# Differential attention: halving the softmax difference first and turning it with transposing DMAs instead of TensorE

## What is computed

```
sc = einsum('bqhtd,bkhtd->bhtqk', qi, k) * HEAD_DIM ** -0.5
p = softmax(where(mask, sc, -inf), axis=-1)
attn = p[:, :, 0] - lam * p[:, :, 1]
o = einsum('bhqk,bkhe->bqhe', attn, v)
```

## Time and profile before

| | us |
|---|---|
| median of 3 runs (lowest to highest) | 1940.49 (1938.78 to 1941.45) |
| the profiled execution, its own time | 1941.98 |
| its span, first to last instruction | 1940.2 |
| granted TensorE clock, mean | 0.999 of full |
| PE busy | 1914.1 (99%) |
| DVE busy | 1180.9 (61%) |
| ACT busy | 996.3 (51%) |
| POOL busy | 389.1 (20%) |

### The profile page before, as it was taken

One profiled execution on the slowest core, in us unless ns is written; L12 is line 12 of the kernel. 1 busy time (PEld: TensorE's weight loads), 2 busy tenths in 40 slices (PEclk: granted clock), 3 DMA queues, 4 the chain that ended last, 5 costly groups with the idle time before them and its releaser, 6 DMA issues.

```text
span 1940.2 us, 28236 instructions
## 1 busy us (share of the span) xinstructions
PE 1914.1 (99%) x11272; PEld 1044.9 (54%) x11272; DVE 1180.9 (61%) x1555; ACT 996.3 (51%) x1924; POOL 389.1 (20%) x266
## 2 busy tenths in 40 slices
PE   7999999999999999999999999999999999999998
PEld 4446755455455665544454576554554556655443
DVE  6677555587436877644367765655872477775432
ACT  5674454465324666533356644544662256665321
POOL 0212011142212232111001130112331222321110
PEclk9999999999999999999999999999999999999999
DMA  6224223343334443233222242233333443332421
GB/s 190 86 87 153 98 98 109 98 117 96 103 103 126 125 126 109 88 130 137 66 66 87 77 163 94 103 109 91 111 104 109 125 115 105 114 109 88 156 93 44
DMA packets 204525, 208.98 MB, mean 108 GB/s; under 512 B 28688, under 2 KB 193514, under 8 KB 204394
## 3 DMA queue, kind: packets, MB, share of 16 engines
q1 hardware_dynamic: 204394, 207.17, 33.9%
HBM read 181.91 MB, written 2.16 MB: 95 GB/s over the span
## 4 chain that ended last, share of the span: by engine, by line
PE 91%; DVE 3%; issue 2%; ACT 1%; DMA 1%; POOL 1%; SPq 0%; DVEq 0%; POOLq 0%; ACTq 0%
PE PS L558 89%; DVE X L1315 1%; PE PS L750 1%; PE PS L666 1%; DVE wsp L1312 1%; DMA stage<-w_in 1%; PE PS L798 0%; PE PS L806 0%; POOL X L1672 0%; PE PS L836 0%; DMA X<-X 0%; DVE Y L1312 0%; DVE Y L1471 0%; ACT Y L1210 0%; DVE M L1312 0%
## 5 line engine op out<-in xcount | busy, mean ns | idle before, releaser
L558 PE MATMUL PS<-hT,wsp 128*128 128x512 f16 (+2 forms) x4968 | 1085.7, 376 | 1.0 <-ACT hT L966 1.0
L558 PEld LDWEIGHTS PS<-hT,wsp 128*128 128x128 f16 x4968 | 479.1, 98 | 556.4 <-issue 11.9
L1312 DVE SCALAR_TENSOR_TENSOR wsp<-stage,wsp 128x2048 f16<-128x2048 f32 x148 | 352.9, 2385 | 165.5 <-ACT wsp L985 163.3
L558 PE MATMUL PS<-ys,wsp 128*128 128x512 f16 x1536 | 340.4, 379 | 0.0
L985 ACT ACTIVATE wsp<-stage 128x2048 f16<-128x2048 f32 x148 | 281.3, 1901 | 50.6 <-PE PS L558 46.9
L558 PEld LDWEIGHTS PS<-ys,wsp 128*128 128x128 f16 x1536 | 149.4, 98 | 177.0 <-issue 4.1
L558 PE MATMUL PS<-wsp,hT 128*128 128x256 f16 x1728 | 194.2, 273 | 0.0
L558 PEld LDWEIGHTS PS<-wsp,hT 128*128 128x128 f16 x1728 | 168.5, 98 | 22.7 <-issue 2.3
L988 ACT ACTIVATE X<-PS 128x512 f32<-128x512 f32 (+1 forms) x120 | 68.5, 594 | 143.4 <-PE PS L558 122.9
L1672 POOL TENSOR_TENSOR X<-X,K 128x1024 f32<-128x1024 f32 x26 | 63.8, 2452 | 365.5 <-DMA X<-X 365.5
L1001 ACT ACTIVATE G<-PS,halfA 128x512 f32<-128x512 f32 x64 | 43.9, 686 | 161.2 <-PE PS L558 119.1
(11 more groups left out here) (199 smaller groups left out, 2056.9 us busy)
## 6 DMA issues: line engine op xcount, KB each, us to landing
stage<-w_in SPq DMA_DIRECT2D x120, 1024.0 KB, 4.9
stage<-w_branch SPq DMA_DIRECT2D x32, 1024.0 KB, 5.0
X<-X SPq DMA_DIRECT2D x120, 128.0 KB, 2.3
stage<-w_out SPq DMA_DIRECT2D x8, 1024.0 KB, 5.4
Y<-sums SPq DMA_DIRECT2D x8, 512.0 KB, 5.8
M<-sums SPq DMA_DIRECT2D x8, 512.0 KB, 5.7
Y<-Y SPq DMA_DIRECT2D x24, 128.0 KB, 2.3
xres<-x SPq DMA_DIRECT2D x4, 512.0 KB, 6.5
```

The costliest lines, as they stand in the source:

```text
L558: return pe.matmul(o, a, b, start=start, stop=stop, skip_group_check=True)
L1312: return dve.scalar_tensor_tensor(out=o, in0=a, scalar=c, in1=b, op0=op0, op1=op1)
```

## The change

The softmax difference is no longer turned on PE. DVE writes the difference in place over E0. ACT makes its f16 high half (`differences_hi`) and DVE the low half (`differences_lo`) in its own layout, side by side in `dH`, 2(i + 1) blocks of 128 x 128. SP turns both halves of a pair with one transposing DMA (`turn_differences`) into `dPT`, from which PE reads. The place of the steps moves as well: `differences_hi` stands before the evacuation of tile (p, 0) on ACT, `differences_lo` directly behind `split_lo` on DVE, and `turn_differences(p)` in SP's iteration p + 2, between the stack of panel p - 2 and the swap of panel p. `dPT` and `dH` hold one pair per e. So a turn waits for the value product of the pair two before (`df_o`), the high half waits for the turn two before (`df_turned`), the next Exp waits for the low half (`df_lo`), and the next scores wait only for the Exp (`df_e`). The exact tile places of `between` and `middle` on PE in these slots go from 12 and 15 to 8 and 12, where nothing is left to do in `between`.

```diff
-        dA = Y[:, 2048:3072].rearrange("p (e n) -> p e n", e=2)
-        dPT = Y[:, 3072:4096].bitcast(F16).rearrange("p (e h n) -> p e h n", e=2, h=2)
+        dH, dPT = (Y[:, a:a + 1024].bitcast(F16).rearrange("p (e n) -> p e n", e=2) for a in (2048, 3072))
...
+                def turn_differences(p):
+                    for e in range(2):
+                        n = 2 * (p - DIFF0) + e
+                        halves = 2 * (n % 4 + 1) * P
+                        sp.wait_ge(s["df_hi"], at("df_hi", n + 1, layer))
+                        sp.wait_ge(s["df_lo"], at("df_lo", n + 1, layer))
+                        if n >= 2:
+                            sp.wait_ge(s["df_o"], at("df_o", n - 1, layer))
+                        sp.dma_start_transpose(dPT[:, e, 0:halves].rearrange("p (b n) -> p b n", n=P), dH[:, e, 0:halves])\
+                            .then_inc(df_turned[e], 16)
...
+                    if DIFF0 <= p - 2 < DIFF0 + 16:
+                        turn_differences(p - 2)
                     if PANELS[p - 2][0] in ROTATED:
...
                             if n >= 2:
-                                pe.wait_ge(s["df_Tl"], at("df_Tl", n - 1, layer))
+                                pe.wait_ge(s["df_e"], at("df_e", n - 1, layer))
...
-                            pe.wait_ge(s["df_Tr"], at("df_Tr", n + 1, layer))
...
-                            pe.wait_ge(s["df_Tl"], at("df_Tl", n + 1, layer))
+                            else:
+                                pe.wait_ge(s["df_or"], at("df_or", n - 1, layer))
+                            pe.wait_ge(df_turned[e], at("df_turned0", 16 * (n // 2 + 1), layer))
...
+                def differences_hi(p):
+                            act.wait_ge(s["df_a"], at("df_a", n + 1, layer))
+                            if n >= 2:
+                                act.wait_ge(df_turned[e], at("df_turned0", 16 * (n // 2), layer))
+                            copy(dH[:, e, 0:nk], dE[:, e, 0, 0:nk]).then_inc(s["df_hi"], 1)
...
-                            tt(dPT[:, e, 1, 0:nk], PS[:, 4 + 2 * e, 0:nk], dPT[:, e, 0, 0:nk], ALU.subtract).then_inc(s["df_Tl"], 1)
+                            dve.wait_ge(s["df_hi"], at("df_hi", n + 1, layer))
+                            tt(dH[:, e, nk:2 * nk], dE[:, e, 0, 0:nk], dH[:, e, 0:nk], ALU.subtract).then_inc(s["df_lo"], 1)
```

More of the change, by code:

```diff
@@ L143, in product_steps @@
 def product_steps(p):
-    if DIFF0 <= p < DIFF0 + 16:
-        return 12, 15
     if PANELS[p][0] == "ga":
@@ L347, in program @@
                  "ssd_ss", "ssd_norm", "ssd_T", "yb_hi", "yb_lo", "sw_vE", "sw_s", "sw_m", "sw_e", "sw_n", "sw_T",
-                 "sw_Ta", "sw_o", "sw_y", "lam_e", "df_s", "df_m", "df_e", "df_a", "df_T", "df_Tr", "df_Tl", "vd_hi", "df_o", "df_or",
+                 "sw_Ta", "sw_o", "sw_y", "lam_e", "df_s", "df_m", "df_e", "df_a", "df_hi", "df_lo", "df_turned0", "df_turned1", "vd_hi", "df_o", "df_or",
                  "df_sq", "df_n", "df_nT", "df_y", "m_acc", "m_hi", "m_lo", "out_sq", "fin_sum", "fin_ss", "x_new",
@@ L353, in program @@
         seg_in = [s["seg_in0"], s["seg_in1"]]
+        df_turned = [s["df_turned0"], s["df_turned1"]]
         x_in = [s["x_in0"], s["x_in1"], s["x_in2"], s["x_in3"]]
@@ L744, in between @@
                         last.then_inc(s["ssd_out"], 1)
[L745 to L751, removed]
                 def local_out(p):
@@ L819, in values @@
                                 pe.wait_ge(s["df_e"], at("df_e", n + 3, layer))
-                            pe.wait_ge(s["df_Tl"], at("df_Tl", n + 1, layer))
+                            else:
+                                pe.wait_ge(s["df_or"], at("df_or", n - 1, layer))
+                            pe.wait_ge(df_turned[e], at("df_turned0", 16 * (n // 2 + 1), layer))
                             for b in range(i + 1):
[L822 to L825, removed]
+                                o, chans = PS[:, 5 + 2 * e, 0:P], slice(P * u, P * u + P)
+                                high, low = (dPT[:, e, P * k:P * k + P] for k in (b, b + i + 1))
+                                mm(o, high, vD[h2 % 2][:, 0, b, chans], b == 0, False)
+                                mm(o, high, vD[h2 % 2][:, 1, b, chans], False, False)
+                                last = mm(o, low, vD[h2 % 2][:, 0, b, chans], False, b == i)
                             last.then_inc(s["df_o"], 1)
@@ L1057, in exponentials @@
                             act.wait_ge(s["df_m"], at("df_m", n + 1, layer))
+                            if n >= 2:
+                                act.wait_ge(s["df_lo"], at("df_lo", n - 1, layer))
                             act.activation(dE[:, e, 0, 0:nk], PS[:, 4 + 2 * e, 0:nk], ACT.Exp, bias=dm[:, e, 0:1], accum_out=dsum[:, e, 0:1])
@@ L1130, in between @@
                             .then_inc(s["dec_ready"], 1)
[L1131 to L1138, removed]
                 def middle(p):
@@ L1164, in middle @@
                             copy(Y_HI[1][:, f, :], PS[:, 4 + t, :], colB[:, B_NG + f:B_NG + f + 1]).then_inc(s["yb_hi"], 1)
+                def differences_hi(p):
+                    if DIFF0 <= p < DIFF0 + 16:
+                        for e in range(2):
+                            n = 2 * (p - DIFF0) + e
+                            nk = (n % 4 + 1) * P
+                            act.wait_ge(s["df_a"], at("df_a", n + 1, layer))
+                            if n >= 2:
+                                act.wait_ge(df_turned[e], at("df_turned0", 16 * (n // 2), layer))
+                            copy(dH[:, e, 0:nk], dE[:, e, 0, 0:nk]).then_inc(s["df_hi"], 1)
                 def value_out(p):
@@ L1242, in one_layer @@
                     before(p)
+                    differences_hi(p)
                     evacuate(p, 0)
@@ L1468, in before @@
                             link(tt(drin[:, e, 1:2], drin[:, e, 1:2], nlam, ALU.mult))
[L1469 to L1472, removed]
+                            link(dve.tensor_scalar(dE[:, e, 0, 0:nk], dE[:, e, 0, 0:nk], drin[:, e, 0:1], None, ALU.mult))
+                            stt(dE[:, e, 0, 0:nk], dE[:, e, 1, 0:nk], drin[:, e, 1:2], dE[:, e, 0, 0:nk], ALU.mult, ALU.add).then_inc(s["df_a"], 1)
                 def local_gated(p):
@@ L1575, in rotated, with differences_lo @@
                         tt(rcos, rcos, rswap, ALU.add).then_inc(s["rope_done"], 1)
-                def turned_low(p):
+                def differences_lo(p):
                     if DIFF0 <= p < DIFF0 + 16:
@@ L1615, in one_layer @@
                             split_lo(n)
+                    differences_lo(p)
                     evacuate(p, 0)
@@ L1622, in one_layer @@
                     middle(p)
-                    turned_low(p)
                     if p > 0:
```

3 lines of the change are left out of this document (1 added, 2 removed).

## The result

| | before | after |
|---|---|---|
| median, us (lowest to highest, 4 runs each) | 1939.86 (1938.78 to 1941.45) | 1927.04 (1926.23 to 1927.49) |
| ratio, 95% interval | | 0.9934 (0.9918 to 0.9950) |
| the profiled execution, own time | 1941.98 | 1926.96 |
| its span | 1940.2 | 1925.2 |

The kernel became faster by 0.66%, 12.8 us by the medians and 15.0 us by the two profiled executions. In the first batch of experiments the same kernel stood at 1926.42 against 1941.56 (0.9926, 0.9914 to 0.9939). The forecast was 1922 us; its range ran from 1918.6, rounded down, to 1940.

The account below looks back on a forecast made before the run. PE was taken to bound the kernel, busy 99% of the span. From 1941.98 us, 17.6 and 2.6 were subtracted, giving 1921.8 (1920.3 from the median); with about 1.7 given back, the forecast was 1922 us, range 1918.6, rounded down, to 1940.

Parts of the forecast that it names:

- The bound: In the two differential attention stretches PE's own instructions are the path; PE is busy 99% of the span.
- the first term: 160 f32 transposes leave PE, 0.77 us per heavy and 0.33 us per light slot, 16 each: 17.6 us saved.
- The second term: PE's waits on DVE at slot starts go, as scores no longer need the turned low half: 2.6 us at most.
- The price of a turn: Transposing DMAs on SP: a heavy pair lands about 3.5 us after issue by bytes, hidden under the panel's matmuls, costing nothing.
- Rival 1: Turns priced by the block land late, PE waits ahead of the value product: slower, 1952 to 1969 us or about 2090; chance 0.13.
- small new delays at the rotated panels and at the ends of heads: Allowance for new delays at these places, about 1.7 us given back from the savings.
- From PSUM or from SBUF, I take them at the same price: Copies and subtractions on ACT and DVE cost the same from either memory; both heavy-slot low halves took 1.23 us.
- rival 2: SBUF-only low halves on DVE stretch beside POOL, light-slot turns come late: 5 to 20 us back, 1927 to 1942; chance 0.10.
- SP's room of 6.7 us: In a heavy slot the turns may hold SP 6.7 us ahead of the rotated panel's swap before PE waits.
- The queue behind the light turns: On SP a panel load behind the light turns goes out about 2 us later, wanted only in the slot after the next.

Follow-up runs that it names:

- e5: The kernel before with one PE transpose per pair instead of one per block (64 of 160 stay): 1932.30 us, 0.9958 of before.
- e1: The changed kernel with DVE's low halves of the difference ahead of the panel's low half (split), not behind it: 1922.99 us, 0.9910 of before.
- e4: The changed kernel with the second turn of every heavy slot issued again after it has landed: 1964.11 us, 1.0119 of before.
- e2: The changed kernel with DVE's low halves at the old place, behind the slot's first evacuation: 1942.40 us, 1.0007 of before.
- e7: The changed kernel with the rotated panel's swap issued by ACT instead of SP in the attention slots: 1952.47 us, 1.0066 of before.
- e3: The changed kernel with plain DMAs of the same bytes in place of the transposing ones, so nothing is turned: 1925.03 us, 0.9923 of before.
- e0: The changed kernel run again, unaltered, as base of comparison: 1926.42 us, 0.9926 of before.
- e12: e1 with the second turn of each heavy slot issued again after landing: 1934.21 us, 0.9966 of before.
- e8: e1 with SP's stack DMAs of a kd panel placed ahead of the panel load: 1924.04 us, 0.9917 of before.
- e10: e2 with SP's stack DMAs of a kd panel placed ahead of the panel load: 1938.33 us, 0.9991 of before.

## Why the prediction was right, and where it was off

- **The bound and the first term (17.6 us off PE)** held. Start by start, the places of the transposes are worth 17.5 us between the traces of before and after, and e5 shows the same price on its own.
- **The second term (2.6 us)** held: no matmul waits for a low half at a slot start any more. The four places were worth 3.3 us, a little more than the idle time that was read.
- **The price of a turn** was right in its conclusion, off in size. For a heavy pair I had 3.5 us by bytes. The pair at 653.43 took 4.4 us, because the second turn goes out 1.3 us behind the first. One turn holds SP 1.2 us, twice the 0.6 of a plain one, and from 2 to 8 blocks its landing grows only from 2.35 to 3.17 us. Rival 1, priced per block, falls. For its two prices from the Trainium skill: 1309 ns per block ("VectorE: DVE Perf Modes", section "The three transpose paths") would be, as an estimate, 10.5 us for eight blocks one after another, and no turn took over 4.5. The 261 GB/s of "DMA: Bandwidth & Descriptors", section "Latency and other measured facts", is near what the growth gives: 192 KB more in 0.8 us, about 240 GB/s as an estimate.
- **The term that was off** is what was given back: 1.7 us "for small new delays at the rotated panels and at the ends of heads". PE lost about 5.6 us in new or longer waits, in two main parts.
- **The first part, 3.0 us, start by start,** is the step "From PSUM or from SBUF, I take them at the same price". It was rival 2, with its mechanism as written (low halves in SBUF beside POOL, 2.55 instead of 0.61 us) and its sign (low halves over 2 us and PE behind them), but with another victim: not the turn comes late, but the row maxima behind the low halves, and through the Exp the value product. Its chance of 0.10 was too low, its price of 5 to 20 us too high, since only four light slots were hit. I had argued that POOL would move behind the low halves. It stayed where it was, 0.04 us after the end of the split before (640.90 against 640.86) and 0.05 after (641.21 against 641.16). e1 takes this part away.
- **The second part, 2.3 us,** lies at the ends of heads, where the value product waited for the same Exp before, only shorter. The norm of the head and the row maxima stand ahead of that Exp on DVE. In one such slot the norm took 2.60 us where it had taken 1.59, in the two others with a wait 1.22. What lengthened the waits stays open.
- **SP's room of 6.7 us** was wrong: e4 held SP that long and lost 2.4 us per heavy slot. It had been counted from the moment at which DVE was free in the trace of before. In the changed kernel the turns were issued 2.2 and 2.8 us later than that, and DVE already waited 2.9 us for POOL.
- **Luck** has a share: rival 2 came true in part, and the time still lies inside the 1918 to 1928 of the forecast. POOL came 0.1 us after the low halves in four slots and 0.2 us after them in eight. Had all twelve been like the four, at 0.75 us each, the time would be about 1933, as an estimate.
- **The queue behind the light turns** was called free, "wanted in the slot after the next". For the load that is so. But the small stack of the next iteration stands behind that load and has next to no room: 0.7 us in the changed kernel, and in e2 7.2 us of waits.

## What to carry to other kernels

When work leaves the bounding engine, look at what the step becomes on the others: an operand moved from PSUM to SBUF made two short DVE operations together four times as long where POOL ran beside them, and the place in the engine's order was worth 19 us from worst to best (e2 to e1) with the same instructions. A DMA put into a queue is paid by what stands behind it, so follow the queue to the next small transfer that somebody waits for; a small transfer right behind a 1 MB one landed after 7.7 us instead of 2.3. Moving a small transfer to another engine's queue did not protect it from a large one in e7, and cost that engine its issue.

## What the runs showed of the hardware that I had not expected

- A transposing DMA from SBUF to SBUF costs nearly the same for 2 to 8 blocks of 128 x 128 f16: 1.20 to 1.25 us of SP and 2.35 to 3.17 us to landing in the medians. That is 0.7 and 0.6 us more than a plain copy of the same bytes (e3).
- Two DVE operations of 128 and 256 columns, SBUF to SBUF, took 2.55 us together when POOL started 0.12 to 0.13 us after the first (four slots). When POOL started 0.19 us after it (eight slots) they took 0.6 us, and POOL's own first operation took 2.4 us instead of 2.14. With one operand in PSUM they took 0.6 us beside POOL in all 12 slots of before.
- Behind the same 2.2 us of idle PE, with the same matmuls, the granted clock fell to half for 3.4 us in the profiled executions of e0, e1, e3, e5, e7 and e12, which cost PE 1.7 us, and stayed full in those of before, after, e2, e8 and e10.
- Four 32-partition DMAs issued by ACT while SP issued a 1 MB load took 3.5 us to issue in the slot shown, against 2.5 us on SP.
